# The second slab of a projection, split for three-pass products in four pieces inside an attention or whole behind it

## The reference

```
xn = rms_norm(h, norm1_g)
proj = xn @ w_in                       # split into the inputs of all four branches
y_a = spatial_gating(gelu(sg_u), gelu(sg_v), ...)      # inputs sg_u, sg_v
y_b = gated_linear_attention(g_q, g_k, g_v, g_r, g_a, ...)
y_c = band_chunk_attention(a_q, a_k, a_v, rel_bias)    # 8 heads of width 64, keys in a band
y_d = conformer_conv(c_a, c_g, ...)    # c_a * sigmoid(c_g), causal convolution of 31 taps,
                                       # layer norm over channels, silu
merged = sum over n of sigmoid(xn @ w_gate[n] + b_gate[n]) * (y_n @ w_branch[n])
h = h + merged @ w_out
```

## Time and profile before

| | |
|---|---|
| median of 3 runs | 2024.95 us (2024.86 to 2025.35) |
| the profiled execution | 2024.88 us |
| its span, first to last instruction | 2022.7 us |
| PE busy in it | 1996.9 us, 99% |
| DVE busy | 1136.2 us, 56% |
| ACT busy | 814.5 us, 40% |
| mean granted TensorE clock | 0.999 of full speed |
| the attention alone on PE | 1129 to 1158 us |

### The profile page before, as it was taken

How to read it: one execution, slowest core, us unless ns; L and a number is a source line. 1 busy time by engine, 2 the same in 40 slices (tenths; PEclk the granted TensorE clock), 3 DMA queues, 4 the chain that set the end, 5 groups by cost and what they waited for, 6 DMA issues and landing times.

```text
span 2022.7 us, 23761 instructions
## 1 busy us (share of the span) xinstructions
PE 1996.9 (99%) x9734; PEld 1647.6 (81%) x9734; DVE 1136.2 (56%) x1618; ACT 814.5 (40%) x1162; POOL 111.9 (6%) x120
## 2 busy tenths in 40 slices
PE   8999999999999999999999999999999999999998
PEld 7887788878888888888888687888888888888886
DVE  6847657566544675366378878733435444234346
ACT  5647633456323333133342635532333333123145
POOL 0004300221000000000010400000000000000000
PEclk9999999999999999999999999999999999999999
DMA  4320022221423332332343132222322233232232
GB/s 134 106 83 22 22 84 92 96 63 63 146 86 102 84 104 96 91 105 81 107 125 105 42 94 84 84 96 92 104 92 96 84 104 101 87 114 96 92 106 82
DMA packets 164441, 184.45 MB, mean 91 GB/s; under 512 B 6759, under 2 KB 125798, under 8 KB 164334
## 3 DMA queue, kind: packets, MB, share of 16 engines
q1 hardware_dynamic: 161006, 175.03, 27.2%
q10 hardware_dynamic: 2624, 5.78, 0.9%
q0 software_dynamic: 704, 2.13, 0.3%
HBM read 180.81 MB, written 2.12 MB: 90 GB/s over the span
## 4 chain that ended last, share of the span: by engine, by line
PE 95%; DVE 3%; ACT 1%; issue 1%; DMA 0%; POOL 0%; DVEq 0%; SPq 0%; ACTq 0%; POOLq 0%
PE ps L453 29%; PE ps L455 29%; PE ps L454 29%; PE ps L580 2%; PE ps L615 1%; PE ps L596 1%; PE ps L650 1%; PE ps L839 1%; ACT HH L1388 0%; DMA W<-in_w_in_dram 0%; DVE arena L2695 0%; DVE arena L2103 0%; PE ps L827 0%; DVE HL L2023 0%; DVE WL L1906 0%
## 5 line engine op out<-in xcount | busy, mean ns | idle before, releaser
L1906 DVE TENSOR_TENSOR WL<-W,WH 128x2048 fp32r<-128x2048 f32 (+2 forms) x162 | 367.6, 2271 | 356.5 <-ACT WH L1338 356.1
L453 PE MATMUL ps<-HH,WH 128*128 128x512 f32 (+1 forms) x1464 | 560.1, 383 | 2.6 <-DVE HL L2023 2.6
L455 PE MATMUL ps<-HH,WL 128*128 128x512 f32 (+1 forms) x1464 | 557.1, 381 | 0.0
L454 PE MATMUL ps<-HL,WH 128*128 128x512 f32 (+1 forms) x1464 | 557.0, 380 | 0.0
L1338 ACT ACTIVATE WH<-W 128x2048 fp32r<-128x2048 f32 (+2 forms) x163 | 307.2, 1886 | 275.4 <-DMA W<-in_w_ff_dram 115.2
L453 PEld LDWEIGHTS ps<-HH,WH 128*128 128x128 f32 x1464 | 276.2, 189 | 56.7 <-issue 2.6
L455 PEld LDWEIGHTS ps<-HH,WL 128*128 128x128 f32 x1464 | 276.2, 189 | 52.4
L454 PEld LDWEIGHTS ps<-HL,WH 128*128 128x128 f32 x1464 | 276.4, 189 | 51.7 <-issue 0.2
L453 PE MATMUL ps<-WH,arena_r 128*128 128x512 f32 (+1 forms) x616 | 238.4, 387 | 0.0
L455 PE MATMUL ps<-WH,arena_r 128*128 128x512 f32 (+1 forms) x616 | 238.4, 387 | 0.0
L454 PE MATMUL ps<-WL,arena_r 128*128 128x512 f32 (+1 forms) x616 | 238.3, 387 | 0.0
(11 more groups left out here) (376 smaller groups left out, 2275.1 us busy)
## 6 DMA issues: line engine op xcount, KB each, us to landing
W<-in_w_in_dram SPq DMA_DIRECT2D x50, 1024.0 KB, 5.2
W<-in_w_ff_dram SPq DMA_DIRECT2D x32, 1024.0 KB, 5.1
W<-in_ffn_w_up_dram SPq DMA_DIRECT2D x44, 512.0 KB, 5.0
W<-in_w_gate_dram SPq DMA_DIRECT2D x16, 1024.0 KB, 5.0
W<-in_ffn_w_down_dram SPq DMA_DIRECT2D x10, 1024.0 KB, 5.0
W<-in_w_out_dram SPq DMA_DIRECT2D x8, 1024.0 KB, 5.0
W<-in_w_branch_dram SPq DMA_DIRECT2D x8, 1024.0 KB, 5.1
W<-in_w_br_ssm_dram SPq DMA_DIRECT2D x4, 1024.0 KB, 5.0
```

The source lines that it names most:

```text
L453: pe.matmul(out_, st[0], mv[0], start=first, stop=False)
L454: pe.matmul(out_, st[0], mv[1], start=False, stop=False)
L455: return pe.matmul(out_, st[1], mv[0], start=False, stop=last)
L1906: dve.tensor_tensor(WL[:, j % RING, 0:n], W[:, j % RING, 0:n], plain(WH[:, j % RING, 0:n]), ALU.subtract).then_inc(slab_lo, 1)
```

## The change

The second "sv" slab is no longer split in quarters in passes 8 to 12. ACT splits it whole in its last pass (18), behind its last copy of turned weights; DVE in its last pass (20), behind its last output copy. Of the 12 taps of pass 17, six stay there and six follow DVE's split in pass 20. PE's instructions, the order of the slabs and all loads are as before.

```
@@ ACT, act_band, beside_scores(step)
-                    if 8 <= step < 12:
-                        split_piece(slab_of["sv", 0, 0], step % 4)
+                    if step == STEPS + LAG - 1:
+                        split(slab_of["sv", 0, 0])

@@ DVE, dve_band, beside_scores(step)
-                    if 9 <= step < 13:
-                        split_piece(slab_of["sv", 0, 0], (step - 1) % 4)
                     if step == STEPS + 1:
-                        taps(12)
+                        taps(6)
+                    if step == STEPS + LAG + 1:
+                        split(slab_of["sv", 0, 0])
+                        taps(6)
```

## The result

The changed kernel takes 2030.55 us (median of 9 runs, 2029.81 to 2032.04) against 2024.87 us before (9 runs, 2023.26 to 2025.53): a ratio of 1.0031, with a 95% interval of 1.0022 to 1.0039. It is slower by 5.7 us, where the forecast was +3.7 us and most of the chance lay on a change within 0.2%. The profiled execution took 2029.87 us, with a span of 2027.7 us, 5.0 longer than before.

The account below looks back on a forecast made before the run. TensorE was taken as the bound, busy 1996.9 of 2022.7 us. A delay of 4.18 less a gain of 0.45 gave +3.73 us, span 2026.4, forecast 2028.7 us, range 2027.0 to 2030.7; within 0.2% had chance 0.69.

Parts of the forecast that it names:

- The quarters: In the attention: removing the split's quarters gains PE 0.13 + 0.22 + 0.10 = 0.45 us, bounds 0 to 0.9.
- the first two: In the attention: the first two quarters fill gaps where DVE waits for PE's scores, so they are free.
- Rival 1: In the attention: the 0.45 us are scatter between turns and nothing is given back, 2029.1 us; chance 0.14.
- The split behind the attention: At the second "sv" slab: PE waits about 0.2 us and loses 0.11 on the first matmul, not a term of the sum.
- The taps: DVE ends the stage 6.23 us later; slack 2.21 at the second "su" slab, so PE loses 4.18 us there.
- Rival 3: Behind the last output copy: DVE's 4.56 us wait for ACT covers the delay, 2024.8 us, no change; chance 0.06.
- rival 4: After the attention: PE's later waits of 1.1 and 0.3 us shrink to nothing, 2027.3 us; chance 0.07.
- at the pace of before: Behind the wait at the second "su" slab: matmuls run as fast as before; half the pace would refute the prediction.
- rival 2: Behind the wait at the second "su" slab: the clock falls and costs 1.9 us, 2030.6 us; chance 0.08.
- the last load: Last of ACT's loads before the turned spatial weights: taking 6.4 us, it makes PE wait up to 1.9 us.
- the other case: At the turned spatial weights: if the last load lands in 4 us, PE has no wait for it.

Follow-up runs that it names:

- e7: Changed kernel, but ACT splits the second "sv" slab in pass 16, DVE in pass 17 ahead of all 12 taps, nothing behind the last output copy: 2024.38 us, ratio 0.9995.
- e1: Changed kernel, but all 12 taps stay in pass 17 and none stands behind the split in pass 20: 2025.05 us, ratio 1.0000.
- e2: Kernel before, quarters kept in the attention, only six of the twelve taps moved from pass 17 to pass 20: 2026.82 us, ratio 1.0010.
- e4: Changed kernel with one wait added on PE, ahead of the turning of the spatial weights, for the third of 12 taps there: 2028.64 us, ratio 1.0020.
- e8: Changed kernel with 12 more matmuls of 512 columns on PE just ahead of the second "su" slab, result not used: 2028.27 us, ratio 1.0017.
- e5: Changed kernel, but with 7 taps in pass 17 and 5 behind the split in pass 20: 2029.20 us, ratio 1.0022.
- e6: Changed kernel, but with 3 taps in pass 17 and 9 behind the split in pass 20: 2030.84 us (5 runs), ratio 1.0035.
- e3: Changed kernel, but six of the 12 taps ahead of the split of the second "su" slab stand behind it: 2025.20 us, ratio 1.0002.

## Why the prediction was wrong

The delay was right step by step, and a term was missing from the sum: the fall of the clock, put at nothing.

- **The quarters.** Forecast 0.45 us, measured 0.49. Of the first two the text said that they are free. That holds for DVE's halves (its next work starts at 1144.56 and 1146.65 us before, at 1144.56 and 1146.64 after), but not for ACT's: its copy for the second quarter stood at 1144.87, ahead of the copy of turned weights that the set of 28 at 1146.92 waits for, which now starts at 1146.38 and not at 1146.59. That is the piece of 0.13 us; the other two come with the last two quarters. Rival 1 (scatter) falls by the intervals under e7.
- **The split behind the attention.** Forecast: PE starts on the second "sv" slab 0.2 us late and loses 0.11 us on the first matmul. In the trace it does, at 1173.41 with a first matmul of 0.50 us. By e1 the split without the taps costs no more than the gain.
- **The taps.** Forecast 6.23 us of delay, a slack of 2.21 us, a wait at the second "su" slab until 1199.5. Measured: 5.70 us net of the gain, and 1199.50. Rival 3 (the delay is covered) falls with ACT's first load issue at 1177.45 and with e2, rival 4 (given back later) with the sum of 5.00 us above.
- **The step that failed** is the sum itself, which let PE run behind the wait "at the pace of before" and put the fall of the clock aside as rival 2, with a chance of 0.08. The rows said only that no wait of that length was in the trace, which is no evidence that the clock stays up. The term measures 1.3 us in the trace (1.45 less 0.11 for the first matmul). e4 and e8, which keep the delay and take away the long idle piece, measure what the forecast gave: +3.67 and +3.69 us in the traces, +3.9 and +3.5 in the medians, against +3.73. The forecast of 2028.7 lay 0.3 us from the border of 2029.0, so this one term decided between no change and slower.
- **Where luck comes in.** The sum with rival 2 was 2030.6 and the median is 2030.55, but its fall of 1.9 us was 0.6 too long against this trace. The traces account for +5.0 us; in the medians (5.7, and 1.7 to 2.2 us for the clock against e4 and e8) the rest is scatter of a kernel whose runs differ by 3 us. That the lower pace of the earlier trace rows is the lower level of the clock is borne out by the changed kernel: 0.21 us for 256 columns there, 0.43 for 512 here at 0.50 granted.
- **A bound taken too wide** helped rival 2 down: the last load was allowed up to 6.4 us, which would have broken the wait in two. It took 4.2 us after the change, and the slab load that shared the DMA engines with it before took 5.1 us instead of 8.3. Loads issued from 1171 to 1185 us in the changed kernel, KB and us to landing:

```profile
W<-in_w_in_dram SPq DMA_DIRECT2D x1, 1024.0 KB, 5.1
...
arena<-in_sg_b_dram ACTq DMA_DIRECT2D x1, 256.0 KB, 4.2
```

In the changed kernel the slab's load is issued at 1173.41 and has landed before ACT's last load goes out; before the change the two were issued at 1173.90 and 1173.66 and ran at the same time. The prediction named 4 us as the other case and gave neither a reason nor a weight. The Trainium skill, DMA: Bandwidth & Descriptors, section Issuing engines are not separate DMA queues, says that DMAs of different issuing engines run on the same 16 engines and interleave; the two times agree with that, though no experiment varied it alone.

The rule of the Trainium skill that the prediction had set aside (TensorE: Matmul & The Clock Gate, section Why this matters for your kernels), that idle gaps between bursts of matmuls take the clock back, came true: the trace agrees, with 0.50 granted after a wait of 3.56 us, and after one of 2.89 us in e5.

## What to carry to other kernels

Work that is moved out of a hidden place should be followed to the end of its engine's stage, not just to its own reader: here the slab split behind the attention was nearly on time for its reader, and what was late was another slab, two hand-offs later, behind a boundary. When TensorE gets an idle piece of a length that was followed by a fall here (2.89 to 4.06 us), give the clock a term in the sum and not only a rival's chance; between 1.69 and 2.89 us nothing was tried. If the wait can't be avoided, two short ones can cost less than a long one (3.67 against 5.00 us here). Filler work of an engine cost nothing ahead of its wait (the taps before the last output copy, e7) and 1.9 us between the wait and a boundary that others are waiting for (e2). And where whole runs scatter by more than the effect, compare traces from an instruction ahead of the change on.

## What the runs showed of the hardware that wasn't expected

Waits of PE and the granted clock behind them, one trace each: 0.82 us (e8), 1.67 us (e2), and 1.69 and 1.65 us twelve microseconds apart (e4) left it at 1.00; 2.89 us (e5), 3.56 us (the changed kernel) and 4.06 us (e6) were followed by a stretch at 0.50. That stretch began while PE was idle in the changed kernel, about as PE started in e5, and some 0.8 us after it had started in e6. So the fall isn't tied to the first matmul after the wait. It cost 1.3 us where it began during the wait and 1.6 us in the two others, where all of it fell on matmuls.

The clock also falls in one place where the view shows no wait of PE. In the traces of e7, e3 and e8, and in none of the other seven, the granted clock falls some 3 us after PE has turned to small products early in the kernel. PE's timeline in e7, then the slices of 1 us:

```profile
56.90 0.43 PE L696 MATMUL ps<-ident,arena 32*128 32x32 f32 x4
57.26 1.95 PE L704 MATMUL ps<-ones,arena 128*128 128x1 f32 x16
59.06 0.42 PE L453 MATMUL ps<-WH,arena_r 128*128 128x384 f32 x1
```

```profile
59.00:60.00 1.00, 1.00 (x7) 1.00 (x8) 0.49 (x3) 0.16 (x2) 0.00 (x0) 1.00 1.02 383
60.00:61.00 1.00, 1.00 (x6) 1.00 (x5) 0.78 (x3) 1.00 (x2) 0.00 (x0) 0.56 1.05 410
61.00:62.00 1.00, 1.00 (x5) 1.00 (x4) 1.00 (x3) 0.93 (x2) 0.00 (x0) 0.50 0.28 105
```

From 56.90 to 59.06 us PE is counted as busy, with four transposes of 32 columns and 16 products of one column. All ten kernels have these instructions, so that they bring the fall about is a guess; it wasn't tried. What the fall costs is plain: from the first of these transposes to the first set of 28 matmuls in the attention it takes 1081.86 to 1081.91 us in the three traces with it and 1080.24 to 1080.34 in the seven without, 1.6 us.

A second source of scatter lies ahead of that. The lower pace of the earlier trace rows lasts for some 20 matmuls in the traces of before and after, for 16 in that of e1, for 7 or 8 in those of e8 and e3, and for one or two in the others, in the same row of instructions. The transposes above start between 56.32 and 57.91 us. At this place the view of the granted clock can't be relied on: it shows 1.00 for every slice from 13 to 18 us of before, where the pace says half. The two together account for most of the spread between 1136.61 and 1138.94 us, at which the ten traces reach the attention. They also mean that a median of this kernel can't show 0.5 us, and that the intervals within a trace had to.
